# Rotary embedding of a two-layer decoder trunk: the half-head exchange by SBUF transfers instead of a TensorE product

## The chip, the cores and the metric

One core of a Trainium2 chip runs the whole program in one launch. The metric is the device time of one execution in microseconds (us), here the median of several executions. Engines are called as the profile calls them: PE (TensorE matmul) and PEld (its weight loads), DVE (VectorE), ACT (ScalarE), POOL (GpSimd), SP (SyncE); SPq and ACTq are the DMA issues that SP and ACT make.

## What is computed

Two layers of a hybrid decoder on a sequence of 256 tokens, D_MODEL 1024, all in float32. Each layer projects x by one matrix `w_in`, feeds three token mixers (a short convolution, attention with rotary positions, an RWKV-7 delta rule), gates and sums them, projects by `w_out`, normalises, and adds a feed-forward part (dense in layer 0, eight experts with the top two per token in layer 1). What matters here is the rotary step on the queries and the keys, eight heads of 64 channels each:

```python
def rope(x, pos):                       # x: (B, T, heads, 64)
    half = HEAD_DIM // 2                # 32
    inv = ROPE_THETA ** (-jnp.arange(half) / half)
    ang = pos[:, None] * inv[None, :]
    cos, sin = jnp.cos(ang), jnp.sin(ang)
    x1, x2 = x[..., :half], x[..., half:]
    return concatenate([x1 * cos - x2 * sin, x2 * cos + x1 * sin], -1)
```

Every channel needs its partner 32 channels away in the same head, times a sine, with a minus sign in the first half of the head.

## The kernel before, in words

**Layout.** Activations of the mixers lie with channels on the partitions and tokens along the free dimension, so a tile of 128 partitions holds two heads, and the two halves of a head are two neighbouring quarters of 32 partitions. Queries and keys are the tiles 0 to 7 of `share` ([128, 12, 256]); a step of the rotary embedding treats two tiles, `share[:, 2s:2s+2, :]` (128x512), and there are four steps, s = 0 to 3, in each of the two layers.

**Projections.** A float32 product is made of three products of fp32r parts: `mm3` (L503 to L505) multiplies high by low, low by high and high by high. The weights of each unit (128x2048) come by two SP loads into one of three `raw` buffers; ACT copies them to `w_hi` (`split_hi`, L1292), DVE subtracts to get `w_lo` (`split_lo`, L1801), and PE may then use them. SP loads the next unit into a `raw` buffer when its `w_lo` is made.

**The order of the work.** It is written out by hand in `TIMELINE` (L138 to L178), a list of steps such as ("front", "qkv", 2). Each engine walks the same list and runs its own handler for a step, if it has one; PE, DVE and ACT each work strictly in that order and meet by semaphores. "front" and "back" are the two halves of one projection unit on PE; on ACT "front" is `split_hi` of the unit two further on and, for gate-like units, the copy of the first bank; "back" copies the result out of PSUM. On DVE "front" is `split_lo` of the unit two further on (for ("qkv", 3) it is in "back", `LATE_LOW`, L181). Between these halves lie the small steps of the mixers. Those near the change:
- `decayed(1)` (ACT L1419, two copies into `ar`), at the end of the line of qkv unit 1.
- `mean(0)` and `var(0)` of the RWKV group norm: PE L895; DVE L1990 centres (`centred`), after that line's `split_lo`; ACT L1440 squares (`ysq_ready`); PE L730 sums the squares in `var`; ACT L1445 takes the root, DVE L1996 the reciprocal; `scaled(0)` is PE L739 (spreads it over channels) and DVE L2003, L2006, L2010.
- `bonus(1)`: DVE L1934, then ACT L1453.
- `scores(1, c)`: PE L783, whose second half, c = 1, waits for the first DVE masks (L1946) of c = 0; four L1946 on DVE for each c. `compact(1)`: ACT L1465, two copies, after the eighth mask.
- `att_scores(0)`: PE L933 and L935, which wait for `rope_ready` of the fourth rotary step; DVE L2025 follows.

**The rotary step.** PE (L913 to L921): one product of `rot` (a 128x128 matrix of 0, 1 and -1 in the constants) with the 128x512 of `share`, in float32, into the PSUM bank `E`. It waits for the rotary step before (bank `E` and its reader), the first for `tok_ready`. DVE (L2012 to L2019): `t4` = `E` times sine (L2017), `share` = `share` times cosine (L2018), sum (L2019), which counts `rope_ready`. ACT has no part in it. The buffers `t1`, `t2`, `t4` (128x512 each: `t_a`, `t_r`, `t_g` in the profile) are those of the RWKV rates and decays; `t4` is last read in `prep(1)` on DVE, `t1` and `t2` in `decayed(1)` on ACT.

**Waits on ACT.** Each `wait_ge` stands on its own before the instruction; a `dma_start` on ACT is issued from the same instruction stream as ACT's activations.

## Time and profile before

| what | value |
|---|---|
| median of 3 runs | 1683.87 us (1683.61 to 1684.73) |
| profiled execution: span, first to last instruction | 1682.6 us |
| its own time | not listed apart from the span |
| PE busy | 1656.3 us, 98% of the span, 10650 matmuls |
| PEld / DVE / ACT / POOL busy | 83% / 76% / 60% / 0% |
| mean granted TensorE clock | 0.993 of 2.4 GHz |
| DMA queue of SP / ACT | 400.97 MB / 8.82 MB |

How to read it: PE is busy nearly throughout, so time is gained where PE does less or waits less, and lost where something makes PE wait. Busy shares of the other engines are averages over stages with different limits and say little about one place; for that the chain of waits and the order of time around the place are read. The rotary steps lie at 180 to 206 us (layer 0) and 713 to 739 us (layer 1).

### The profile page before, as it was taken

The page shows a single profiled execution, that of the slowest core. Times are in us where ns is not written, and L with a number is a line of the kernel's source. Part 1 is how long each engine was busy: PE and PEld are TensorE (multiplying, and loading weights), DVE is VectorE, ACT ScalarE, POOL GpSimd, SP SyncE. Part 2 cuts the span into 40 slices and gives each one's busy share as a digit, 9 for nine tenths or more (in the row PEclk, how much of TensorE's full clock was granted, in tenths as well). Part 3 has the DMA queues.
Part 4 walks back from the last instruction along what each step waited for, and adds up shares of the span by engine and source line. Part 5 has one row for each costly group of instructions (what it writes and reads, how often), then busy time and mean ns, then how long its engine had stood idle before and what let it go on. Part 6 is the DMA issues. An engine that isn't in the chain of part 4 may idle for free.

```text
span 1682.6 us, 27509 instructions
## 1 busy us (share of the span) xinstructions
PE 1656.3 (98%) x10650; PEld 1402.5 (83%) x10650; DVE 1273.1 (76%) x1226; ACT 1001.9 (60%) x968; POOL 2.9 (0%) x12
## 2 busy tenths in 40 slices
PE   9999999999999999999999999999999999999997
PEld 8988788778887998978888888888888888888885
DVE  5766775664446668496478899898988889898987
ACT  6554463454444645444446777777776777777775
POOL 0000000000000000000000000000000000000000
PEclk9999999999999999999998999999999999999999
DMA  9433333556564543334376999999999999998993
GB/s 295 137 116 126 125 126 101 204 166 199 175 199 150 188 144 109 113 125 127 101 255 236 364 353 384 325 373 330 393 336 373 364 335 394 328 367 322 392 374 143
DMA packets 216185, 411.04 MB, mean 244 GB/s; under 512 B 9376, under 2 KB 83488, under 8 KB 215584
## 3 DMA queue, kind: packets, MB, share of 16 engines
q1 hardware_dynamic: 213840, 400.97, 67.5%
q10 hardware_dynamic: 2256, 8.82, 1.4%
q8 instruction: 63, 1.03, 0.3%
q14 instruction: 26, 0.21, 0.0%
HBM read 407.66 MB, written 2.10 MB: 244 GB/s over the span
## 4 chain that ended last, share of the span: by engine, by line
PE 93%; DVE 4%; issue 1%; ACT 1%; DMA 0%; SPq 0%; DVEq 0%; ACTq 0%
PE W L503 20%; PE W L505 19%; PE W L504 19%; PE Y L503 7%; PE Y L504 7%; PE Y L505 7%; PE Y L796 4%; PE W L701 1%; DVE w_lo L1801 1%; PE Y L701 1%; PE Y L783 1%; PE E L708 0%; DMA raw<-w_in 0%; PE Y L1072 0%; PE Y L1073 0%
## 5 line engine op out<-in xcount | busy, mean ns | idle before, releaser
L503 PE MATMUL W<-w_lo,x_hi 128*128 128x512 f32 (+1 forms) x1168 | 452.8, 388 | 1.5 <-DVE x_lo L2115 0.9
L505 PE MATMUL W<-w_hi,x_hi 128*128 128x512 f32 (+1 forms) x1168 | 442.2, 379 | 0.0
L504 PE MATMUL W<-w_hi,x_lo 128*128 128x512 f32 (+1 forms) x1168 | 441.5, 378 | 0.0
L1801 DVE TENSOR_TENSOR w_lo<-raw,w_hi 128x2048 fp32r<-128x2048 f32 x112 | 256.5, 2291 | 174.0 <-ACT w_hi L1292 172.7
L1808 DVE TENSOR_TENSOR w_lo<-raw,w_hi 128x2048 fp32r<-128x2048 f32 x144 | 329.6, 2289 | 45.6 <-ACT w_hi L1298 45.6
L1298 ACT ACTIVATE w_hi<-raw 128x2048 fp32r<-128x2048 f32 x144 | 276.1, 1917 | 72.6 <-PE Y L505 40.0
L1808 DVE TENSOR_TENSOR w_lo<-raw_more,w_hi 128x2048 fp32r<-128x2048 f32 x120 | 275.0, 2291 | 28.3 <-ACT w_hi L1298 27.6
L1298 ACT ACTIVATE w_hi<-raw_more 128x2048 fp32r<-128x2048 f32 x120 | 230.5, 1921 | 64.8 <-PE W L505 42.0
L1292 ACT ACTIVATE w_hi<-raw 128x2048 fp32r<-128x2048 f32 x112 | 214.2, 1913 | 81.6 <-PE W L505 47.8
L503 PEld LDWEIGHTS W<-w_lo,x_hi 128*128 128x128 f32 x1168 | 219.9, 188 | 45.0 <-issue 4.5
L505 PEld LDWEIGHTS W<-w_hi,x_hi 128*128 128x128 f32 x1168 | 219.7, 188 | 42.0
L504 PEld LDWEIGHTS W<-w_hi,x_lo 128*128 128x128 f32 x1168 | 220.1, 188 | 39.4 <-issue 1.0
L503 PE MATMUL Y<-w_lo,o_hi 128*128 128x512 f32 x440 | 172.2, 391 | 0.7 <-DVE o_lo L2128 0.7
L504 PE MATMUL Y<-w_hi,o_lo 128*128 128x512 f32 x440 | 171.3, 389 | 0.0
L505 PE MATMUL Y<-w_hi,o_hi 128*128 128x512 f32 x440 | 171.3, 389 | 0.0
L503 PE MATMUL W<-x_lo,w_hi 128*128 128x256 f32 x536 | 157.4, 294 | 3.0 <-DVE w_lo L1791 2.5
L504 PE MATMUL W<-x_hi,w_lo 128*128 128x256 f32 x536 | 152.0, 284 | 0.0
L505 PE MATMUL W<-x_hi,w_hi 128*128 128x256 f32 x536 | 151.9, 283 | 0.0
L503 PEld LDWEIGHTS W<-x_lo,w_hi 128*128 128x128 f32 x536 | 103.0, 192 | 7.1 <-issue 3.6
L504 PEld LDWEIGHTS W<-x_hi,w_lo 128*128 128x128 f32 x536 | 103.1, 192 | 0.3
L505 PEld LDWEIGHTS W<-x_hi,w_hi 128*128 128x128 f32 x536 | 103.1, 192 | 0.0
L503 PEld LDWEIGHTS Y<-w_lo,o_hi 128*128 128x128 f32 x440 | 82.6, 188 | 17.6 <-DVE w_lo L1801 1.2
(332 smaller groups left out, 1853.3 us busy)
## 6 DMA issues: line engine op xcount, KB each, us to landing
raw<-w_in SPq DMA_DIRECT2D x123, 512.0 KB, 4.6
raw<-moe_gate SPq DMA_DIRECT2D x48, 1024.0 KB, 6.4
raw<-moe_up SPq DMA_DIRECT2D x48, 1024.0 KB, 7.0
raw<-moe_down SPq DMA_DIRECT2D x48, 1024.0 KB, 5.7
raw_more<-moe_gate SPq DMA_DIRECT2D x40, 1024.0 KB, 7.5
raw_more<-moe_up SPq DMA_DIRECT2D x40, 1024.0 KB, 7.1
raw_more<-moe_down SPq DMA_DIRECT2D x40, 1024.0 KB, 6.3
raw<-w_branch SPq DMA_DIRECT2D x24, 512.0 KB, 4.5
```

The costliest lines, as they stand in the source:

```text
L503: nc.tensor.matmul(out_ap, lhs[0], rhs[1], start=start, stop=False)
L504: nc.tensor.matmul(out_ap, lhs[1], rhs[0], start=False, stop=False)
L505: return nc.tensor.matmul(out_ap, lhs[0], rhs[0], start=False, stop=stop)
L701: return nc.tensor.transpose(out_ap, in_ap, ident)
L783: last = nc.tensor.matmul(Y[(1 + u + h) % 4][:, part], keys[rows, m, tc], ar[rows, m, c].rearrange("p s t -> p (s t)"), start=True, stop=True)
L796: last = nc.tensor.matmul(tiles(bank, 4)[half, u, :], left[half, 4 * c + u, :], right[half, 4 * c + u, :], start=True, stop=True)
L1292: A(w_hi[u % 3][:], raw[u % 3][:], ACT.Copy).then_inc(hi_done, 1)
L1298: A(w_hi[(u + x) % 3][:], landing(place_of(x))[:], ACT.Copy).then_inc(hi_done, 1)
L1801: V.tensor_tensor(w_lo[u % 3][:], raw[u % 3][:], w_hi[u % 3][:].bitcast(F32), ALU.subtract)\
L1808: V.tensor_tensor(w_lo[r][:], landing(place_of(x))[:], w_hi[r][:].bitcast(F32), ALU.subtract).then_inc(lo_done, 1)
```

## The change

PE's `rope` goes. ACT gets a step `swap(s)`, four per layer, each with four SBUF to SBUF transfers of 32 partitions by 512 float32 (64 KB each): quarter i of the buffer `SWAPPED[s]` gets quarter i^1 of `share[:, 2s:2s+2, :]`. DVE's `rope` multiplies that buffer by the sine in place (no PSUM bank any more), and the minus sign is put once, in layer 0, step 0, into the sine table: two instructions on 32 partitions by 256. `swap(0)`, `swap(1)`, `swap(2)` and `swap(3)` stand in the list after `decayed(1)`, before `var(0)`, before ACT's `split_hi` of ("front", "qkv", 4), and before that of ("front", "qkv", 5).

```diff
@@ TIMELINE
-    ("front", "qkv", 1), ("cu", 0, 1), ("back", "qkv", 1), ("cy", 0, 1), ("yrow", 0), ("decayed", 1),
-    ("front", "qkv", 2), ("mean", 0), ("back", "qkv", 2), ("var", 0), ("tok", 1),
-    ("front", "qkv", 3), ("scaled", 0), ("bonus", 1), ("back", "qkv", 3), ("rope", 0), ("scores", 1, 0),
-    ("front", "qkv", 4), ("scores", 1, 1), ("compact", 1), ("back", "qkv", 4), ("rope", 1),
+    ("front", "qkv", 1), ("cu", 0, 1), ("back", "qkv", 1), ("cy", 0, 1), ("yrow", 0), ("decayed", 1), ("swap", 0),
+    ("front", "qkv", 2), ("mean", 0), ("back", "qkv", 2), ("swap", 1), ("var", 0), ("tok", 1),
+    ("front", "qkv", 3), ("scaled", 0), ("bonus", 1), ("back", "qkv", 3), ("swap", 2), ("rope", 0), ("scores", 1, 0),
+    ("front", "qkv", 4), ("scores", 1, 1), ("compact", 1), ("back", "qkv", 4), ("rope", 1), ("swap", 3),
@@ shared by the engines
+        SWAPPED = (t4, t1, t2, t4)
+        QUARTERS = [slice(a, a + HD // 2) for a in range(0, P, HD // 2)]
@@ tensor engine
-            def rope(l, s):
-                wait_jobs(pe, l * MIX_JOBS + JOB0["qkv"] + s + 1)
-                if s:
-                    pe.wait_ge(sem("rope_ready"), 4 * l + s)
-                else:
-                    pe.wait_ge(sem("tok_ready"), 2 * l + 2)
-                nc.tensor.matmul(E[:], rot, share[:, 2 * s:2 * s + 2, :].rearrange("p m t -> p (m t)"),
-                                 start=True, stop=True).then_inc(sem("rot_done"), 1)
@@ scalar engine
+            def swap(l, s):
+                wait_jobs(act, l * MIX_JOBS + JOB0["qkv"] + s + 1)
+                if s < 3:
+                    act.wait_ge(sem("decayed_ready"), 2 * l + 2)
+                    act.wait_ge(sem("prep_ready"), 2 * l + 2)
+                else:
+                    act.wait_ge(sem("rope_ready"), 4 * l + 1)
+                for i, to in enumerate(QUARTERS):
+                    act.dma_start(SWAPPED[s][to], share[QUARTERS[i ^ 1], 2 * s:2 * s + 2, :]).then_inc(sem(f"swapped{s % 3}"), 16)
@@ vector engine, rope(l, s)
-                dve.wait_ge(sem("rot_done"), 4 * l + s + 1)
-                V.tensor_tensor(t4[:], tiles(E[:]), sin, ALU.mult)
+                other = SWAPPED[s]
+                if l == 0 and s == 0:
+                    dve.wait_ge(sem("cst_full"), 96)
+                    for quarter in QUARTERS[0::2]:
+                        last = V.tensor_scalar(cst[quarter, C_SIN:C_END], cst[quarter, C_SIN:C_END], -1.0, None, ALU.mult)
+                    link(last)
+                dve.wait_ge(sem(f"swapped{s % 3}"), 64 * (l + 1) if s in (1, 2) else 64 * (2 * l + 1 + s // 3))
+                V.tensor_tensor(other[:], other[:], sin, ALU.mult)
                 link(V.tensor_tensor(src, src, cos, ALU.mult))
-                mark(V.tensor_tensor(src, t4[:], src, ALU.add), "rope_ready", 4 * l + s + 1)
+                mark(V.tensor_tensor(src, other[:], src, ALU.add), "rope_ready", 4 * l + s + 1)
```

## Rows read from the trace of the kernel before

**Rows 1.** The page, part 4: the chain that ended last, shares by engine.
```profile
PE 93%; DVE 4%; issue 1%; ACT 1%; DMA 0%; SPq 0%; DVEq 0%; ACTq 0%
```

**Rows 2.** PE in order of time, second rotation: start us, us, engine, line, operation.
```profile
190.97 0.39 PE L505 MATMUL W<-w_hi,x_hi 128*128 128x512 f32 x1
191.20 1.02 PE L920 MATMUL E<-share,cst 128*128 128x512 f32 x2
...
192.29 0.40 PE L504 MATMUL W<-w_hi,x_lo 128*128 128x512 f32 x1
```

**Rows 3.** Chain of waits, 177 to 188 us: start us, us, what.
```profile
177.00 0.70 DVE mc L2003
...
180.08 2.29 DVE w_lo L1801
...
184.33 0.70 DVE sc L1946
...
187.26 1.13 PE Y L783 x8
```

**Rows 4.** DVE in order of time, 195 to 202 us; brackets: idle before, releaser.
```profile
195.66 2.29 DVE L1801 TENSOR_TENSOR w_lo<-raw,w_hi 128x2048 fp32r<-128x2048 f32 x1 [1.30 <-ACT w_hi L1292]
...
201.15 2.29 DVE L1801 TENSOR_TENSOR w_lo<-raw,w_hi 128x2048 fp32r<-128x2048 f32 x1 [1.28 <-ACT w_hi L1292]
```

**Rows 5.** PE in order of time, the first attention scores.
```profile
206.02 0.49 PE L933 MATMUL Y<-share 64*128 64x128 f32 x4 [1.07 <-DVE share L2019]
```

**Rows 6.** ACT and its DMA issues (ACTq) in order of time, 861 to 863 us.
```profile
861.81 0.59 ACT L1529 ACTIVATE x_hi<-W 128x512 fp32r<-128x512 f32 x1
861.84 0.38 ACTq L1535 DMA_DIRECT2D xtok<-x_spill  x1
862.26 0.49 ACTq L1537 DMA_DIRECT2D cmo<-const_moe  x1
862.28 1.92 ACT L1292 ACTIVATE w_hi<-raw 128x2048 fp32r<-128x2048 f32 x1
862.78 0.45 ACTq L1538 DMA_DIRECT2D rt_s<-router  x1
```

**Rows 7.** SP's issues in order of time: a run of small loads.
```profile
15.34 0.62 SPq L382 DMA_DIRECT2D cm<-const  x1
```

**Rows 8.** ACT in order of time, 163 to 170 us.
```profile
163.83 0.62 ACT L1419 ACTIVATE ar<-t_r 128x512 f32<-128x512 f32 x1
164.35 1.90 ACT L1292 ACTIVATE w_hi<-raw 128x2048 fp32r<-128x2048 f32 x1
169.33 0.63 ACT L1440 ACTIVATE xn<-mc 128x512 f32<-128x512 f32 x1 [3.08 <-DVE mc L1990]
```

**Rows 9.** DVE in order of time: the same split in layer 0 and in layer 1.
```profile
166.28 2.29 DVE L1801 TENSOR_TENSOR w_lo<-raw,w_hi 128x2048 fp32r<-128x2048 f32 x1 [7.73 <-ACT w_hi L1292]
...
699.56 2.29 DVE L1801 TENSOR_TENSOR w_lo<-raw,w_hi 128x2048 fp32r<-128x2048 f32 x1 [7.73 <-ACT w_hi L1292]
```

**Rows 10.** PE's weight loads in order of time: the sums of squares in `var(0)`.
```profile
170.15 0.98 PEld L730 LDWEIGHTS Y<-cst,xn 128*128 128x128 f32 x8
```

**Rows 11.** ACT in order of time, 170 to 176 us: the root of `var(0)`.
```profile
172.38 0.27 ACT L1445 ACTIVATE inv<-Y,small 128x8 f32<-128x8 f32 x1
```

**Rows 12.** ACT in order of time, 181 to 194 us.
```profile
181.37 1.90 ACT L1292 ACTIVATE w_hi<-raw 128x2048 fp32r<-128x2048 f32 x1
192.34 1.27 ACT L1465 ACTIVATE ac<-sc 64x512 f32<-64x512 f32 x2 [9.07 <-DVE sc L1946]
193.64 1.92 ACT L1292 ACTIVATE w_hi<-raw 128x2048 fp32r<-128x2048 f32 x1
```

**Rows 13.** DVE in order of time: a pair of scalar products over 256 columns.
```profile
141.06 0.62 DVE L1921 TENSOR_SCALAR t_g<-t_g,prm 128x256 f32<-128x256 f32 x2
```

**Rows 14.** DMA issues by line: KB each, median us from issue to landing.
```profile
prm<-par SPq DMA_DIRECT2D x1, 86.0 KB, 8.4
```

**Rows 15.** Busy us by stretch: PE, PEld, DVE, ACT, POOL; granted clock, DMA share, GB/s.
```profile
880.00:890.00 10.00, 10.00 (x49) 8.99 (x49) 7.13 (x18) 8.43 (x10) 0.00 (x0) 0.63 0.00 0
```

More of the change, by code:

```diff
@@ L1229, in _ @@
                         "spread": spread, "tok": tok, "scores": scores, "invert": invert, "mx": mx, "dx": dx, "cg": cg, "cu": cu,
-                        "cy": cy, "mean": mean, "var": var, "scaled": scaled, "rope": rope,
+                        "cy": cy, "mean": mean, "var": var, "scaled": scaled,
                         "att_scores": att_scores, "probs_t": probs_t, "att_out": att_out}
@@ L1706, in _ @@
                         "exps": exps, "ksq": ksq, "knorm": knorm, "decayed": decayed, "tok": tok, "bonus": bonus, "invert": invert,
-                        "mx": mx, "compact": compact, "cg": cg, "cu": cu, "yrow": yrow, "mean": mean, "var": var,
+                        "swap": swap, "mx": mx, "compact": compact, "cg": cg, "cu": cu, "yrow": yrow, "mean": mean, "var": var,
                         "softmax": softmax, "probs_t": probs_t, "att_out": att_out, "osplit": osplit, "msplit": msplit,
```

## The prediction, made before the changed kernel was run

> **What bounds the kernel now.** I read the shares of the chain that ended last first: PE carries 93% of it, DVE 4% [rows 1]. So a change counts where it shortens PE's work on that chain, or where it makes PE wait. The shares cannot say which of the two holds at the rotary steps; that takes the order of time around them. In layer 0 there are two stretches. From 177 to 187 us the chain runs over DVE: `scaled(0)`, the bonus, a weight split, rotary step 0, four masks, and only then PE's second half of `scores(1, 1)` [rows 3]. From there it is PE's own work, with rotations 1 and 2 in it, until the first attention scores, before which PE sat idle for 1.07 us for the fourth rotary sum [rows 5]. Layer 1 repeats this 533.3 us later [rows 9].
>
> **What goes: eight products on PE.** Around rotation 1 the last product before it starts at 190.97 and the second after it at 192.29 [rows 2], 1.32 us apart. Starts of undisturbed products of 512 columns lie 0.23 us apart (190.97 to 191.20 [rows 2]), so two steps would be 0.46, and a rotation costs PE 0.86 us. Eight make 6.9 us, 0.4% of the run. Of these I count:
> - Rotation 0 (both layers): nothing. It stands ahead of `scores(1, 0)`, but PE's next point on the chain, at 187.26, waits for DVE's masks, and those come one after the other on DVE from 177.00 on, with no PE in between [rows 3]. PE only waits longer.
> - Rotations 1 and 2: 2 x 0.86 = 1.72 us earlier on PE, rotation 3 another 0.86; but the next meeting point is the fourth rotary sum on DVE [rows 5]. It hangs on two weight splits with a rotary step between them: 195.66 and 201.15, before which DVE was idle for 1.30 and 1.28 us, waiting for ACT's high part [rows 4]. The first high part (ACT 193.64) comes right after the masks and `compact(1)` [rows 12], so PE's gain does not move it. The second waits for PE's last qkv product, which does come 1.72 us earlier. So the second split can start 1.28 us earlier at most, then DVE is the bound. That is the whole gain on offer: at most 1.28 us a layer, and rotation 3 is worth nothing.
>
> **What comes: sixteen transfers a layer on ACT's stream.** ACT's issues are taken from [rows 6]: 861.84, 862.26, 862.78, and the third ends at 863.23, so 1.39 us for three, 0.46 each; four take 1.84 us. ACT's own next work waits behind them. The same rows say when they start: 861.84 is 0.03 us after the ACTIVATE of 861.81 began, while the next ACTIVATE, earlier in the program than the issues, ran only at 862.28. So issues pass behind work already handed to the engine, and hide under it. Bounds for one issue: 0.38, the first of the run [rows 6], and 0.62, SP in a run of small loads [rows 7]; four, with 0.04 between, make 1.6 to 2.6 us. I take 1.84, ACT's own.
> - **swap(0)** waits for `decayed_ready`, the end of the copy before it, 163.83 + 0.62 = 164.45 [rows 8]. So nothing hides it. The issues run from 164.47 to 166.31, and `split_hi` starts then and not at 164.35: 1.96 us late. Behind it, in order: the split on DVE (it had been idle 7.73 us for this high part [rows 9]), `centred` behind that split, and ACT's square (idle 3.08 us for `centred` [rows 8]), which ended at 169.96. PE began to load these squares as weights at 170.15 [rows 10]. With 0.05 us for the signal the slack is 0.14 us. So PE now stands for 1.96 - 0.14 = 1.82 us in `var(0)`. Nothing takes it back: the chain from there to 177.00 is PE's, then DVE's. Two layers: **+3.64 us**. By the bounds of an issue the stall is 1.6 to 2.6 us.
> - **swap(1)** (1.84 us) stands ahead of the root. The root ran at 172.38 [rows 11]; its reciprocal is first needed by PE's spread about 1.05 us before 177.00 [rows 3], near 175.9. Since PE itself is 1.8 us late, slack is about 2.9 us after 0.5 us for root and reciprocal are in. Hidden; uncovered only if an issue took over 0.7 us.
> - **swap(2)** delays a `split_hi` of 181.37 [rows 12] by 1.84. DVE takes that unit after the four masks, at 187.2 [rows 3]; 1.90 us of work from 183.2 ends at 185.1. Hidden by 2.1 us.
> - **swap(3)** can be issued once the second of the two copies of `compact(1)` is handed over, just after 192.34 [rows 12]: from 192.36 to 194.20. `split_hi` starts 0.56 us later than 193.64. The first split and rotary step 2 go with it, so the gain at the second split is 1.28 - 0.56 = 0.72 us. If the issues start only when the second copy runs, 0.64 later, 0.1 us is left; with issues of 0.62 us, none. Two layers: **-1.44 us**, bounds -1.9 (issues of 1.6 us in all) and +0.2.
> - **Landing.** swap(0) to swap(2) are issued at least 10 us before DVE reads them; swap(3) by 194.20, read at about 203.3. The longest landing of a small transfer, 86 KB, took 8.4 us from issue, in the crowded start [rows 14]; even that fits. No trace row has SBUF as the source. Taken as nothing.
> - SP's queue is not passed by anything; its loads that wait for the late splits move 0.6 to 2 us and have over 10 us to their use. Of the other queues POOL's is untouched.
>
> **The sign.** In layer 0, step 0, DVE does two products on 256 columns and waits for their end, on the chain of [rows 3]. A pair of that kind took 0.62 us [rows 13] on 128 partitions; on 32 I know no row, so 0.4 (if fewer partitions help) to 0.7. Taken 0.65 with the wait: **+0.65 us**, once. The first rotary product now reads SBUF and not PSUM; like its neighbours it is 128x512 and counted as equal.
>
> **Sum.** 3.64 + 0.65 - 1.44 = +2.85 us. The profiled execution has a span of 1682.6; no other time is listed for it, and the median of the runs is 1.27 us above it. What lies around the span does not change, so the sum is added to the median: 1683.87 + 2.85 = **1686.7 us**, +0.17%. A measurement of this kernel tells 0.2% (3.4 us) from no change. The bounds by terms: low 1.6 x 2 + 0.4 - 1.9 = +1.7 (1685.6), high 2.6 x 2 + 0.7 + 0.2 = +6.1 (1690.0).
>
> **A rule that speaks against the stall.** The Trainium skill, "DMA: Bandwidth & Descriptors", section "Issuing engines are not separate DMA queues", says that the time a sequencer takes to start a DMA is usually small beside the DMA itself. Read as a reason to count the issues as nothing, it would take out both the stall and the 0.56 us; [rows 6] and the 0.14 us of slack speak against it here.
>
> **Rivals.**
> - **A: the issues cost ACT nothing.** Then no stall, and the full 1.28 us a layer: 0.65 - 2.56 = -1.9, 1682.0 us. For it: issues do pass behind running work [rows 6]. Against: swap(0)'s own wait leaves ACT empty. Chance 5%.
> - **B: PE gets its 0.86 us back for every rotation,** because DVE's chain is not as tight as it looks: -6.9 + 0.65 = -6.2, 1677.6 us, faster. Against: the two meeting points of [rows 3, 5]. Chance 3%.
> - **C: long issues, slower.** Place: swap(0) in both layers. Small transfers of 32 rows go at 0.62 us an issue as in [rows 7]: four with gaps 2.6 us, stall 2.6, gain of swap(3) gone: +6.0, 1689.9 us. It crosses the 0.2% when an issue takes over 0.49 us (each 0.01 more costs 0.16 over both layers, stall and swap(3) together). For it: so close to 0.46. Chance of being past that point 31%.
> - **D: the clock.** PE's waits grow: 1.8 us in `var(0)`, then products of 2 columns, and before the attention scores from 1.07 [rows 5] to 1.07 + 3 x 0.86 - 0.72 = 2.9 us. In the router stage, where PE ran mostly products of 8 columns, the granted clock averaged 0.63 over 10 us [rows 15], so part of it at the 1.2 GHz level. If one such drop of about 7 us came in each layer, half of it is lost: +7 on top, 1693.7 us. Against: full-width products on either side of both waits. Chance 8%. The Trainium skill, "TensorE: Matmul & The Clock Gate", section "HAM oscillation — how this bites in real kernels", makes idle gaps the cause of such drops; no row here shows a gap alone doing it.
> - **E: the transfers land late or are not used:** a wait on `swapped` before step 3. It decides only if landing takes over 9 us from issue; +0.5 to 2. Chance 3%.
>
> **How the numbers follow.** My forecast, a net of +1.7 to +3.4, has 50%. With most of A and a third of E inside the 0.2% band (1680.5 to 1687.2), no change comes to 0.55; slower (C, D, the rest of E) to 0.41; faster (B and the rest of A) to 0.04. The predicted time is that of the likeliest case, 1686.7. The range for 8 in 10: 1684.0, which leaves A and B out, to 1690.3, which holds C and leaves D out.
>
> **What the profile after would show.** L920 gone, 16 matmul records fewer, 32 new ACTq rows of about 0.4 us. After `decayed(1)` four issues, then `split_hi` near 166.3 and PE's L730 with an idle of about 1.8 us, released by ACT L1440, in both layers. DVE's first mask at 184.33 + 1.8 + 0.65 in layer 0 and without the 0.65 in layer 1. Before L933 PE idle for about 2.9 us, released by DVE's sum, and the distance from the eighth mask to L933 0.7 us shorter. `swapped` never the last releaser. I am wrong if L730 does not wait (A), if the distance from masks to scores shrinks by over 1.28 us (B), if issues last 0.6 us (C), or if the granted clock falls in 170 to 210 us (D).

## The result and the profile after

| | before | after |
|---|---|---|
| median | 1683.74 us (4 runs, 1682.77 to 1684.73) | 1698.53 us (4 runs, 1698.16 to 1698.97) |
| ratio | | 1.0086, 95% interval 1.0073 to 1.0098 |
| span of the profiled execution | 1682.6 us | 1696.8 us |
| mean granted TensorE clock | 0.993 | 0.988 |
| PE busy, matmuls | 1656.3 us, 10650 | 1657.3 us, 10634 |

The change costs 14.8 us, 0.9%. It was forecast at 1686.7 with a range up to 1690.3, so even the range is missed. PE has 16 records fewer and is busy 1 us longer: its work went down and each piece of it took longer somewhere. The page's chain says where else to look: PE fell from 93% to 90%, "issue" rose from 1% to 2%, and ACT's queue from nothing to 1%.

```profile
PE 90%; DVE 5%; issue 2%; ACT 2%; ACTq 1%; DMA 0%; SPq 0%; DVEq 0%
```

The order of time on ACT and its queue, layer 0, answers to [rows 8] and [rows 11]:

```profile
164.40 0.62 ACT L1412 ACTIVATE ar<-t_r 128x512 f32<-128x512 f32 x1
165.21 3.06 ACTq L1501 DMA_DIRECT2D t_g<-share  x4
168.37 1.92 ACT L1285 ACTIVATE w_hi<-raw 128x2048 fp32r<-128x2048 f32 x1 [3.35 <-issue]
...
174.07 1.90 ACTq L1501 DMA_DIRECT2D t_a<-share  x3
176.00 1.28 ACT L1438 ACT_TABLE_LOAD   x1 [1.52 <-issue]
```

The same place in layer 1:

```profile
705.57 0.62 ACT L1412 ACTIVATE ar<-t_r 128x512 f32<-128x512 f32 x1
706.37 2.47 ACTq L1501 DMA_DIRECT2D t_g<-share  x4
708.95 1.92 ACT L1285 ACTIVATE w_hi<-raw 128x2048 fp32r<-128x2048 f32 x1 [2.76 <-issue]
```

Before, `split_hi` started 0.52 us after the start of the second copy [rows 8]. Now it starts 3.97 us after it (164.40 to 168.37): 3.45 us late in layer 0, and by the same reckoning 2.86 in layer 1 (705.57 to 708.95, less 0.52). The four issues are 3.06 and 2.47 us of that. The rest is 0.3 us before the first and 0.1 behind the last.

PE's two longest waits, as the groups of waits have them (engine, result and line <- who was waited for: us in total, times, longest). The one in `var(0)` is new, the one before the attention scores grew from 1.07 us [rows 5]. Below them PE's rows at the wait of `var(0)` in either layer (L733; [rows 10]) and at the attention scores in layer 0 (L926):

```profile
PE Y L926 <- DVE share L2029: 7.9, 2, 4.0
PE Y L733 <- ACT xn L1433: 5.5, 2, 3.1
```

```profile
174.05 1.86 PE L733 MATMUL Y<-cst,xn 128*128 128x2 f32 x8 [3.05 <-ACT xn L1433]
...
179.55 0.41 PE L507 MATMUL W<-x_hi,w_lo 128*128 128x256 f32 x1
179.76 0.41 PE L508 MATMUL W<-x_hi,w_hi 128*128 128x256 f32 x1
...
180.51 0.28 PE L507 MATMUL W<-x_hi,w_lo 128*128 128x256 f32 x1
180.63 0.28 PE L508 MATMUL W<-x_hi,w_hi 128*128 128x256 f32 x1
...
213.56 0.49 PE L926 MATMUL Y<-share 64*128 64x128 f32 x4 [3.96 <-DVE share L2029]
...
714.63 1.05 PE L733 MATMUL Y<-cst,xn 128*128 128x2 f32 x8 [2.46 <-ACT xn L1433]
```

Look at the durations. The eight products at 174.05 take 1.86 us, and those at 714.63 take 1.05. After the first, products of 256 columns start 0.21 us apart until about 180, then 0.12. That is the clock, as the windows of this trace say (the last but two column is the granted clock, in parts of 2.4 GHz; 0.50 is the 1.2 GHz level):

```profile
174.00:180.00 6.00, 5.95 (x22) 4.81 (x23) 0.20 (x1) 2.46 (x4) 0.00 (x0) 0.50 0.70 216
180.00:186.00 6.00, 6.00 (x57) 5.70 (x57) 2.16 (x4) 2.46 (x3) 0.00 (x0) 0.99 0.00 0
214.00:217.00 3.00, 3.00 (x17) 2.06 (x14) 2.44 (x8) 0.00 (x0) 0.00 (x0) 0.54 0.47 180
716.00:719.00 3.00, 3.00 (x12) 2.28 (x11) 0.20 (x1) 1.65 (x3) 0.00 (x0) 0.50 1.00 355
754.00:757.00 3.00, 3.00 (x9) 2.42 (x8) 2.93 (x9) 0.00 (x0) 0.00 (x0) 0.51 0.08 29
```

Four stretches at 1.2 GHz that the trace of before does not have (there the windows 160 to 180, 200 to 220, 700 to 720 and 740 to 760 us all stand at 1.00). Each starts within 1.5 us of the end of one of PE's four waits, the first already in the last 0.7 us of its wait. The first lasts about 7 us, the other three about 3.5. PE is called busy all through them, which is why its busy share hides the loss.

A third wait of PE grew as well, for the masks before the second half of `scores(1, 1)` (L786 here): from 0.2 to 1.25 us in layer 0, which is the "PE only waits longer" of the prediction. No low stretch follows it.

**Where the 14.2 us of span are.** DVE does the same work in both traces, so the distance of a row from its twin before is the delay at that point. Four of DVE's rows, layer 0:

```profile
183.77 0.69 DVE L2007 TENSOR_TENSOR mc<-mc,Y 128x512 f32<-128x512 f32 x1 [5.91 <-PE Y L742]
189.07 0.57 DVE L2024 TENSOR_SCALAR cst<-cst 32x256 f32<-32x256 f32 x2
204.43 2.29 DVE L1805 TENSOR_TENSOR w_lo<-raw,w_hi 128x2048 fp32r<-128x2048 f32 x1 [2.68 <-ACT w_hi L1285]
208.69 2.29 DVE L1805 TENSOR_TENSOR w_lo<-raw,w_hi 128x2048 fp32r<-128x2048 f32 x1
```

- 177.00 [rows 3] is now 183.77, 6.77 late. Of this 0.6 came from the start of the run (it differs by up to 4 us between traces, see below), 3.3 is the stall (3.45 less the slack of 0.14), and the remaining 2.9 is the clock.
- The sign takes 0.6 (189.07 to 189.68): 7.4.
- The second weight split, 201.15 [rows 4], is at 208.69: 7.54. The rotations' removal was to bring it 0.72 forward. It gave nothing, as the split before it now waits 2.68 us, not 1.30, for the high part that stands behind swap(3).
- A split at 232.16 before comes at 240.36: 8.2, and 8.4 further on. So the clock behind the attention scores took about 0.9.
- Layer 1 in the same way: 2.9 for the stall by the split at 710.90 (699.56 before, [rows 9]), so 11.3; 1.5 to 1.7 for the clock by 723.11 (710.28 before), so 12.8; 0.1 by the second split; 1.2 for the clock behind the scores, so 14.2.

Together: stalls 6.0 us, clock 6.7, sign 0.6, the second splits +0.3, start of the run 0.6. The clock's share is a difference between delays, not a row of its own, and the experiments test it. One more place must be kept in mind for them: the router stage (before: about 882 to 897 us) has a low stretch of 14 us in both traces, and the delay is the same ahead of it and behind it, 14.1 and 14.2 us.

### The profile page after: what moved, and what is told of

Read it like the earlier page. It is cut to its first block, busy times and chain, and to the rows that moved or that the text cites. A ratio compares the mean times of both kernels' runs of the same rounds, so it can differ in the third digit from the quotient of the medians.

```text
span 1696.8 us, 27512 instructions
## 1 busy us (share of the span) xinstructions
PE 1657.3 (98%) x10634; PEld 1406.0 (83%) x10634; DVE 1273.9 (75%) x1228; ACT 1002.6 (59%) x968; POOL 2.9 (0%) x12
## 4 chain that ended last, share of the span: by engine, by line
PE 90%; DVE 5%; issue 2%; ACT 2%; ACTq 1%; DMA 0%; SPq 0%; DVEq 0%
PE W L506 19%; PE W L508 18%; PE W L507 18%; PE Y L506 7%; PE Y L508 7%; PE Y L507 7%; PE Y L799 4%; PE W L704 1%; DVE w_lo L1805 1%; DVE sc L1950 1%; ACT w_hi L1285 1%; PE Y L704 1%; ACTq L1501 1%; PE Y L786 0%; PE E L711 0%
```

## The experiments

Each was timed against the kernel before on the same chip; "delay" is again the distance of a DVE row from its twin in the trace of before. Before stood at 1684.08 beside experiments 1, 2, 3 and 8, at 1683.87 beside 5, 6, 7 and 9, and at 1684.21 beside 4, 10 and 11.

**1. No transfers.** DVE multiplies whatever the buffers hold: the exchange of quarters is left out, the three DVE instructions and the sign stay.

```diff
 def swap(l, s):                      # scalar engine
 ...
-                for i, to in enumerate(QUARTERS):
-                    act.dma_start(SWAPPED[s][to], share[QUARTERS[i ^ 1], 2 * s:2 * s + 2, :]).then_inc(sem(f"swapped{s % 3}"), 16)
 def rope(l, s):                      # vector engine
 ...
-                dve.wait_ge(sem(f"swapped{s % 3}"), 64 * (l + 1) if s in (1, 2) else 64 * (2 * l + 1 + s // 3))
+                dve.wait_ge(sem("decayed_ready"), 2 * l + 2)
```

> Leaves the exchange out: no SBUF transfers, the sine multiplies what lies in the buffers; PE's rotations stay gone, the sign stays. My theory after the result: the loss comes from ACT's issues (0.61 us each, not 0.46), which hold PE in var(0) by 3.3 and 2.7 us, and from four stretches at the 1.2 GHz level that follow PE's waits (2.9, 0.9, 1.65 and 1.25 us by the shifts between the two traces). Without transfers no wait in var(0), so 1683.7 + 0.6 (sign) - 2 x 1.28 = 1681.8 us if the clock holds before the attention scores, about 1684 if it falls there. The rival, that the products on PE kept it busy and their removal alone brings the clock down, says: the clock falls in 206 to 220 us here too, and the time is 1684 or more.

Measured: 1684.10 us (10 runs, 1681.99 to 1685.35), ratio 0.9998 (0.9988 to 1.0007). So the sixteen transfers a layer, with all that follows from them, are the whole 14 us (whether it is their issue or their traffic is settled by experiment 8). But the other half is as telling: without transfers the kernel should have been faster by the two times 1.28 us of [rows 4], less the sign. It isn't. The order of time on PE and DVE before the attention scores, layer 0:

```profile
201.52 2.29 DVE L1803 TENSOR_TENSOR w_lo<-raw,w_hi 128x2048 fp32r<-128x2048 f32 x1
...
206.40 0.49 PE L926 MATMUL Y<-share 64*128 64x128 f32 x4 [2.58 <-DVE share L2027]
...
208.86 0.63 PE L507 MATMUL W<-w_hi,o_lo 128*128 128x512 f32 x1
209.28 0.63 PE L508 MATMUL W<-w_hi,o_hi 128*128 128x512 f32 x1
```

The split no longer waits: the delay was 1.60 us on the way there (1.0 of it from the start of the run, 0.6 the sign) and is 0.37 at 201.52, so the gain of 1.23 is there. PE, with 2.6 us less to do, then waits 2.58 us instead of 1.07, and its next products start 0.43 us apart and not 0.23. After that the delay is 1.60 again. Layer 1 does the same: 1.68 ahead of the two splits, 0.43 at the second, 1.73 behind the scores, with a low stretch from 740 to 743.5 us. What DVE gained, the clock took. This is the outcome that the expectation gave to its rival for that place: the removal of the products is enough to bring the clock down there, by way of the longer wait and without any transfer.

**2. The sign in the constants.** Two edits: the two `tensor_scalar` of the vector engine go, and the host lays the table out with its signs.

```diff
-                if l == 0 and s == 0:
-                    dve.wait_ge(sem("cst_full"), 96)
-                    for quarter in QUARTERS[0::2]:
-                        last = V.tensor_scalar(cst[quarter, C_SIN:C_END], cst[quarter, C_SIN:C_END], -1.0, None, ALU.mult)
-                    link(last)
...
-    general = np.concatenate([general, np.tile(np.cos(ang), (4, 1)), np.tile(np.sin(ang), (4, 1))], 1)
+    general = np.concatenate([general, np.tile(np.cos(ang), (4, 1)), np.concatenate([-np.sin(ang), np.sin(ang)] * 2)], 1)
```

> The changed kernel with the minus sign in the constant table and not made by DVE. My theory: exactly the two products (0.57 us and a signal) leave the chain: 1698.5 - 0.6 = 1697.9 us. The rival: at that point PE waits anyway through another path, and nothing changes: 1698.5.

Measured: 1698.68 us (4 runs), ratio 1.0083 (1.0066 to 1.0100), the same as the changed kernel. The 0.6 us are gone from DVE's order, but behind the attention scores of layer 0 the low stretch was twice as long as in the changed kernel:

```profile
211.00:218.00 7.00, 5.00 (x21) 3.79 (x22) 5.73 (x14) 1.32 (x2) 0.00 (x0) 0.54 0.47 150
```

The four issues of layer 0's first group took 2.53 us here and not 3.06, so this trace lacks a second half microsecond, and still ends later. So what was saved on the path was lost again to the clock in this trace. With one trace it can't be said whether that is the rule.

**3. PE kept running in both waits.** Idle products (128x256, into a bank that nobody reads) before either wait, nothing else. They can't take the stall away.

```diff
 def var(l, p):
+                if p == 0:
+                    keep_running(6)
                 pe.wait_ge(sem("ysq_ready"), 2 * l + p + 1)
 def att_scores(l, part):
                 if part == 0:
+                    keep_running(8)
                     pe.wait_ge(sem("rope_ready"), 4 * l + 4)
```

> The changed kernel, with idle products on PE into the free bank E: six ahead of the wait in var(0), eight ahead of the wait for the attention scores (some 0.45 us each, so 2.7 and 3.6 us, inside the waits of 2.5 to 3.1 and 4.0 us). My theory: the waits stay, the clock stays at 2.4 GHz in all four places, and 6.7 us come back: 1691.8 us. The rival, that the slow stretches cost nothing because DVE and ACT are the bound there, says 1698.5 us with the clock high.

Measured: 1690.06 us (7 runs, 1689.33 to 1691.14), ratio 1.0033 (1.0021 to 1.0044): 8.5 us less than the changed kernel, by doing more work on the busiest engine. The windows at the four places, in the same columns as above:

```profile
174.00:180.00 6.00, 5.42 (x39) 4.47 (x38) 0.84 (x2) 3.80 (x7) 0.00 (x0) 1.00 0.77 219
206.00:212.00 6.00, 5.49 (x27) 4.37 (x26) 5.86 (x8) 3.19 (x2) 0.00 (x0) 1.00 0.77 230
707.00:713.00 6.00, 6.00 (x41) 5.46 (x40) 2.98 (x2) 2.18 (x3) 0.00 (x0) 1.00 0.18 40
739.00:745.00 6.00, 6.00 (x28) 5.03 (x27) 5.93 (x5) 3.40 (x4) 0.00 (x0) 1.00 0.46 145
```

This shows the clock's share at the four places: none of the low stretches is left, and ahead of the router stage the delay is 8.5 us, 1.8 of it from the start of the run, against 14.1 with 0.6. That is 6.8 us less, where the sum above has 6.7. The rest of the gain in this trace is not at the four places: in the router stage, whose low stretch was 14 us in before and after and 7 us here, the delay falls from 8.5 to 6.5. So the 6 us by which this kernel is still slower than before are the stalls, the sign and the second splits (6.9 together), less what the router stage gave, with the scatter of the start.

**4. PE kept running at the first place only**, `keep_running(6)` in `var` alone.

> The changed kernel with six idle products on PE ahead of its wait in the first variance product alone. Against the changed kernel (1698.5): if the clock falls only for the wait in front of it, the low stretches at 174 to 181 and 716 to 720 us go (2.9 + 1.65 = 4.5 us), those before the attention scores stay, the stall itself (3.3 + 2.7) stays: median 1693 to 1695. If the two places are coupled, the second goes too and it comes near the 1690.1 with both filled.

Measured: 1695.32 us (4 runs, 1694.95 to 1695.80), ratio 1.0067 (1.0052 to 1.0083), 3.2 us less than the changed kernel and just outside the expected 1693 to 1695. The low stretches behind `var(0)` are gone, and the row of 183.77 stands at 181.00. But in layer 1 PE's wait before the scores grew to 4.74 us and the low stretch behind it from 3.5 to 7 us:

```profile
747.00:753.00 6.00, 4.26 (x19) 3.20 (x20) 4.75 (x11) 0.31 (x1) 0.00 (x0) 0.50 0.52 175
```

It cost 1.9 us of delay there and not 1.2. The two shares don't simply add: filling both is worth 8.5, and the first alone 3.2.

**5. PE's eight products kept**, as products of constants of the same size; the changed kernel else.

```diff
@@ tensor engine; its entry in the list of handlers comes back too
+            def rope(l, s):
+                wait_jobs(pe, l * MIX_JOBS + JOB0["qkv"] + s + 1)
+                if s:
+                    pe.wait_ge(sem("rope_ready"), 4 * l + s)
+                else:
+                    pe.wait_ge(sem("tok_ready"), 2 * l + 2)
+                nc.tensor.matmul(E[:], rot, cst[:, 0:512], start=True, stop=True)
```

> The changed kernel with a product of the same size in the place of each rotation (constants as data, into the idle bank, nobody reads it): transfers, sign and ACT's stream as in the changed kernel, PE's work as before. If PE's freed time is what makes it stand long enough before the attention scores for the clock to fall: the wait there is 1.5 to 2.5 us and not 4.0, no stretch at 1.2 GHz at 214 to 218 and 754 to 757 us; against the changed kernel 0.9 + 1.25 less, and up to 1.3 a layer more for the rotations' own time at the second split: median 1696.5 to 1699. The stall in the first variance product and the clock behind it (3.3 + 2.9 and 2.7 + 1.65 us) stay. If the rotations' removal does not bear on the clock: 1699 or more with the low stretches still there.

Measured: 1693.72 us (4 runs, 1692.71 to 1696.44), ratio 1.0060 (1.0045 to 1.0076), 4.8 us less than the changed kernel and below the expected 1696.5 to 1699. PE's waits and the two places before the attention scores:

```profile
PE Y L733 <- ACT xn L1442: 5.9, 2, 3.4
...
PE Y L935 <- DVE share L2038: 1.8, 2, 0.9
```

```profile
209.00:215.00 6.00, 5.00 (x27) 3.48 (x28) 5.60 (x7) 1.78 (x1) 0.00 (x0) 1.00 0.83 277
743.00:749.00 6.00, 5.91 (x24) 4.05 (x22) 5.93 (x8) 1.95 (x2) 0.00 (x0) 1.00 0.59 185
```

The waits before the scores are 0.9 us and not 4.0, and the clock holds; that is the 2.1 us (0.9 and 1.2) which the low stretches behind them had cost. The second split comes where it came in the changed kernel (209.16 against 208.69, with the delay in front of it 0.5 greater), so eight products more on PE cost nothing there. **At this place the work that was saved on PE was worth less than nothing**: it turned into a wait, and the wait into a lower clock. The rest, and the reason why it came out better than expected, is not due to the eight products as far as is shown. In layer 1 the clock did not fall behind a wait of 2.46 us in `var(0)`, and in the changed kernel it did, behind 2.46 too (some 1.6 us). And in the router stage the delay falls from 10.8 to 8.6 us, with a low stretch of 7 us and not 14.

**6. swap(0) alone moved** on ACT's stream, to where nobody waits closely.

```diff
-    ("front", "qkv", 1), ("cu", 0, 1), ("back", "qkv", 1), ("cy", 0, 1), ("yrow", 0), ("decayed", 1), ("swap", 0),
-    ("front", "qkv", 2), ("mean", 0), ("back", "qkv", 2), ("swap", 1), ("var", 0), ("tok", 1),
+    ("front", "qkv", 1), ("cu", 0, 1), ("back", "qkv", 1), ("cy", 0, 1), ("yrow", 0), ("decayed", 1),
+    ("front", "qkv", 2), ("mean", 0), ("back", "qkv", 2), ("swap", 1), ("var", 0), ("tok", 1), ("swap", 0),
```

> The changed kernel with swap(0) alone moved on ACT's stream, from behind decayed(1) to behind tok(1). If the loss sits in swap(0)'s place: PE's wait in the first variance product is gone (it had 3.05 and 2.46 us), and so is the low clock at 174 to 181 and 716 to 720 us: 6.2 us less in layer 0, 4.3 in layer 1, median near 1688. If every place of four issues costs ACT's readers the same: the stall shows up elsewhere (the root, scaled or the first bonus) and the median stays above 1694.

Measured: 1688.28 us (10 runs, 1686.21 to 1691.52), ratio 1.0026 (1.0017 to 1.0035), as expected to 0.3 us. PE does not wait in `var(0)`, and the clock stands at 1.00 there in both layers. So ten of the 14.8 us went with the place of one group of four issues. That the forecast was so close is partly luck: the low stretch before the scores of layer 1 was 7 us here and not 3.5, and in the router stage the delay fell by 2.5 us (5.7 to 3.2), which no one had counted. What is left is the sign and the attention waits, still 3.95 and 3.94 us (2.58 without transfers, experiment 1), as swap(3) keeps DVE late, with the clock behind them.

**7. Other shapes of transfer**, to find why an issue takes 0.61 us and not 0.46.

```diff
 for i, to in enumerate(QUARTERS):    # step 3 is as it was
+                    c = slice(64 * i, 64 * i + 64)
+                    if s == 0:
+                        a, b = SWAPPED[s][:, :, c], share[:, 2 * s:2 * s + 2, c]
+                    elif s == 1:
+                        a, b = SWAPPED[s][to], w_branch[l, 0:32, 0:512].rearrange("p (m t) -> p m t", m=2)
+                    elif s == 2:
+                        a, b = SWAPPED[s][to, 0, :], share[QUARTERS[i ^ 1], 2 * s, :]
 ...
+                    act.dma_start(a, b).then_inc(sem(f"swapped{s % 3}"), 16)
```

The exchange is left out in steps 0 and 1 and for half of step 2, so this kernel is for the durations of the issues alone.

> The changed kernel with other shapes of its transfers, four a step still: step 0 moves 128 rows by 64 columns of each token half, rows kept (same bytes, four times the rows, a quarter of the run length); step 1 reads 32 rows of the branch weights in HBM and not SBUF; step 2 moves 32 rows but one token half, half the bytes; step 3 is as it was. The exchange is left out in steps 0 and 1 and half of step 2. If an issue's time goes with the number of runs or rows: step 0 over 0.61 us, step 2 under. If it goes with SBUF as source: step 1 under 0.5 and the others 0.6. If it is a constant of ACT's queue in a group of four: all 0.5 to 0.6, and the first 0.46 came from groups of three with work beside them.

Measured: 1698.43 us (one run). The DMA issues of one line, by tile (ns min, median, max), first of the changed kernel, then of this one, with the group of step 0 in layer 1 below:

```profile
L1501 ACTq DMA_DIRECT2D t_g<-share x16: 514/612/1147, 165.2 to 740.4; - x16
L1501 ACTq DMA_DIRECT2D t_a<-share x8: 515/612/614, 173.5 to 715.9; - x8
```

```profile
L1510 ACTq DMA_DIRECT2D t_g<-share x16: 515/626/1337, 165.2 to 741.0; - x16
L1510 ACTq DMA_DIRECT2D t_a<-w_branch x8: 349/441/444, 173.9 to 716.0; - x8
L1510 ACTq DMA_DIRECT2D t_r<-share x8: 595/612/618, 187.3 to 728.8; - x8
...
706.67 2.72 ACTq L1510 DMA_DIRECT2D t_g<-share  x4
```

`t_r`, half the bytes: 0.61 as before. `t_g` mixes step 0, with four times the rows, and step 3, as it was; the group of step 0 in layer 1 took 2.72 us and not 2.47, so the rows added 0.06 us an issue. `t_a`, same destination, same bytes, source in HBM and not SBUF: 0.44, and 0.35 for the first. **With the destination in SBUF the source made the difference.** The rows on which the forecast of 0.46 rested all had HBM as the source.

SBUF as the source is not dear by itself, though. The trace of before has four issues that store from SBUF to HBM, one on ACT and three on SP, at 0.33 to 0.39 us. The one on ACT:

```profile
L1362 ACTq DMA_DIRECT2D x_spill<-xtok x1: 391/391/391, 581.7 to 581.7; - x1
```

The 0.6 us belong, as far as these runs go, to transfers with SBUF at both ends. They are not the only dear ones: SP's small loads of [rows 7], from HBM into 64 partitions, took 0.62 each. What an issue spends the time on is open. What made the fourth issue of layer 0's first group take 1.15 us (1.34 here) is open; SP issued nothing in that time.

**8. SP issues the transfers**, the sign in the table. Swaps 0 to 2 stand behind the load of the second unit of branch 0, swap 3 behind the first of gate 1.

```diff
@@ sync engine; swap itself moves here from the scalar engine, with sp in the place of act
                         for q in range(n):
                             load_rows(u + q, 0, w_branch[l, :, q * 512:(q + 1) * 512], where * BR, BT)
+                            if where == 0 and q == 1:
+                                for s in range(3):
+                                    swap(l, s)
 ...
                             load_rows(u + q, 0, w_in[l][:, c:c + 512], 512 * (q % 2), 4)
+                            if kind == "gate1" and q == 0:
+                                swap(l, 3)
```

> The same sixteen transfers a layer, but issued by SP where it waits anyway (steps 0 to 2 after the load of the second unit of branch0, step 3 after the first of gate1), sign in the table. My theory: ACT's stream is free, no wait in var(0), the transfers land long before DVE reads them: 1683.7 - 2 x 1.28 = 1681.2 us if the clock holds before the attention scores, about 1683.3 if it falls. The rival, that it is the transfers' traffic and landing and not the issuing engine, says it stays near 1698.

Measured: 1683.31 us (10 runs, 1681.58 to 1685.92), ratio 0.9992 (0.9982 to 1.0002). The 14.8 us are gone, and nothing is gained. The same sixteen transfers a layer still run, so their traffic and their landing were not the cost; what cost was that ACT issued them, ahead of work that PE waits for. (0.6 of the 14.8 us is the sign, now in the table.) SP's queue in the order of time:

```profile
171.52 2.49 SPq L407 DMA_DIRECT2D t_g<-share  x4
...
176.77 2.41 SPq L407 DMA_DIRECT2D t_r<-share  x4
184.26 0.38 SPq L352 DMA_DIRECT2D raw<-w_in  x1
```

Four issues take SP 2.4 us too; it has them to spare, since its next load comes 5 us after the last of them. PE waits 2.58 us before the attention scores in both layers. Behind it the clock fell in layer 0 and not in layer 1:

```profile
207.00:210.00 3.00, 3.00 (x18) 2.09 (x17) 1.92 (x6) 0.33 (x1) 0.00 (x0) 0.50 0.48 186
738.00:744.00 6.00, 3.89 (x26) 3.10 (x27) 5.45 (x13) 2.83 (x2) 0.00 (x0) 1.00 0.56 180
```

The delay says what that is worth. In layer 0 it is 1.81 us ahead of the splits, 0.58 at the second, 1.81 again behind the scores: gained and lost. In layer 1, with the same edit and the same wait, it is 2.04, then 0.78, and stays there.

**9 and 10. The same with PE kept running before the attention scores**, `keep_running(8)` and then `keep_running(5)` as in experiment 3.

> The run sp_sign with eight products of 256 columns on PE (0.22 us each, 1.8 us in all) ahead of its wait for the fourth rotary sum, where PE stood for 2.6 us. If the clock gives back the gain of the removed rotations: no stretch at the 1.2 GHz level at 207 to 211 us, the 1.2 us a layer at the second weight split (201.15) are kept through the attention scores, and the median is 1681 to 1682.5, that is 1.5 to 2.5 below sp_sign and the kernel before. If the gain is lost for another reason (DVE's own order, weight loads): no change against sp_sign, 1683 to 1684.

Measured: 1683.45 us (11 runs, 1682.57 to 1685.49), ratio 0.9998 (0.9989 to 1.0007). No low stretch at either place, yet no gain that can be told from none: the size of the filler was wrong in the expectation. Eight products took 3.62 us, 0.45 each, and DVE waited 1.20 us for the first scores where before it was 0.38 (L2025 there), so 0.8 of the 1.24 us was given back.

> sp_sign_fill with five products ahead of the fourth rotary sum and not eight. Eight took 3.62 us (736 to 739.5 us), 0.45 us each and not the 0.22 expected there, and DVE then waited 1.20 us for the first scores in layer 0 where it had waited 0.38 before: they overshot by 0.8 us a layer. Five are 2.26 us, which ends ahead of the sum. If the clock is all that gives the gain back: no low stretch around 207 and 740 us, the first attention scores 1.2 us a layer earlier than in the kernel before, median 1681.0 to 1682.3. If a remaining wait of 0.5 us is enough for the clock to fall, or the gain is lost further on: 1683 to 1684.5, no change.

Measured: 1682.46 us (11 runs, 1680.68 to 1684.58), ratio 0.9986 (0.9977 to 0.9995). The only version whose interval lies below 1, and just above the expected range. PE at the place, and the windows of both layers:

```profile
205.94 2.32 PE L529 MATMUL E<-s_s 128*128 128x256 f32 x10
208.67 0.49 PE L943 MATMUL Y<-share 64*128 64x128 f32 x4 [0.40 <-DVE share L2030]
```

```profile
205.00:211.00 6.00, 5.60 (x35) 4.29 (x34) 5.52 (x10) 3.20 (x2) 0.00 (x0) 1.00 0.74 263
738.00:744.00 6.00, 5.59 (x35) 4.29 (x34) 5.48 (x12) 3.19 (x2) 0.00 (x0) 1.00 0.63 211
```

The delay falls by 1.24 us at the second split in layer 0 and by 1.26 in layer 1 (201.15 and 734.46 before), and stays down both times. That is the 1.28 us a layer of the prediction, reached with the issues and the clock out of the way, and it is read from rows. Neither the span nor the median shows it by itself. This trace, of the slowest of the eleven runs, was 3.9 us late by 67 us, and its router stage gave back 1.9. The median is 1.75 us below that of before, which could hold the gain of the router stage as well as that of the splits. And an interval that ends at 0.9995, one of eleven, is weak evidence that the kernel is faster at all.

**11. The transfers still on ACT**, with the repairs of 2, 3 (second place) and 6 together.

> The changed kernel with its transfers still on ACT's queue: swap(0) behind tok(1), sign in the table, eight idle products ahead of the attention scores. If the shares add up: 1688.3 less 0.6 for the sign less what the low clock at 209 to 212 and 741 to 748 us took, 2 to 4: median 1684 to 1686, so no or a small loss against before. If the clock finds another place (longer low stretch elsewhere, as with the sign alone): 1687 or more.

Measured: 1685.78 us (10 runs, 1684.57 to 1687.33), ratio 1.0010 (1.0000 to 1.0019). Within the expected range: the shares add up here, and what remains of the loss is at the edge of what can be told from none. Before the attention scores the clock stood at 1.00. From 166 us to the router stage the delay grows by only 0.5 us (2.0 to 2.5), and there it falls to 0.3.

## Why the prediction was wrong, point by point

- **What bounds the kernel: right.** The two meeting points held. PE waited in `var(0)` and before the attention scores, for the releasers that were named. PE's own 0.86 us per rotation was worth nothing (experiment 5), and the 1.28 us a layer that were on offer exist (experiments 8 and 10).
- **The term "four take 1.84 us": mis-sized.** Four issues took 2.47 us on ACT (3.06 once) and cost 0.4 more around them. The stall was 3.3 and 2.7 us, not 1.82 each: +6.0 in place of +3.64. The prediction had both prices in front of it, 0.46 and 0.62, and took ACT's own because the engine matched. What mattered was what lies at the two ends (experiment 7), which it touched only for the landing, with "No trace row has SBUF as the source". That is not so: four issues of the trace before read SBUF, at 0.33 to 0.39 us. What no row has is SBUF at both ends. A kind of transfer that no row has makes every price of an issue a bound, not only the one that comes to mind.
- **The gain of 1.44 us: gone, as its own bound said.** "With issues of 0.62 us, none" is what came: the second splits are 0.1 to 0.15 us later per layer.
- **The sign: right**, 0.6 against 0.65.
- **swap(1) and swap(2) hidden, landing nothing: right.** swap(1) holds ACT's load of a function table (ACT_TABLE_LOAD) 1.52 us and does not come up among PE's waits. Landing took 1.9 to 5.1 us from issue. The issuing page of the Trainium skill ("DMA: Bandwidth & Descriptors", section "Issuing engines are not separate DMA queues") calls the issue time usually small beside the DMA; here 0.61 us stands against a landing of 2.1 at the median. It is the smaller of the two, which is of no help: the cost lay in what stood behind the issues on ACT.
- **Rival C had the mechanism and 31%, and 1689.9.** By it alone the kernel would have come to +6.6 or so (stalls 6.0, sign 0.6), near its upper bound of 1690. Experiment 3, with the clock held at the four places, measured 1690.06; some 2 us of the router stage are in that, so the agreement is closer than the reasoning deserves.
- **Rival D is the step that failed.** It was priced as an alternative, at 8%, with "full-width products on either side of both waits" against it. The products are there, and they did not hold the clock. It fell behind both waits, in both layers, and took some 6.7 us in the trace; experiment 3, which held it, won 8.5 us in the medians (6.8 at the four places by its trace). It was also not independent: once the stall is longer, and PE has less work before the scores, both waits grow (to 3.05, 2.46, 3.96 and 3.96 us). D belonged on top of C, and even on top of the forecast itself: that had a wait of 2.9 us before the scores, and in experiment 1 a wait of 2.58 brought the clock down in both layers. With C and D together the prediction's own figures give 1689.9 + 7 = 1697, against 1698.5 measured, a sum made with the result in hand. The rule that was cited beside it (the Trainium skill, "TensorE: Matmul & The Clock Gate", section "HAM oscillation — how this bites in real kernels"), that idle gaps of PE bring such drops, is borne out by experiments 3 and 4, where the filled gaps have no drop behind them. And "no row here shows a gap alone doing it" overlooked the start of the trace before, where a wait of 2.54 us has a low stretch with it, from 12.2 to 15.7 us (PE in order of time, and the window):

```profile
12.54 0.58 PE L503 MATMUL W<-x_lo,w_hi 128*128 128x256 f32 x1 [2.54 <-DVE w_lo L1791]
...
12.00:16.00 4.00, 3.46 (x17) 3.47 (x18) 3.44 (x4) 2.80 (x3) 0.00 (x0) 0.57 1.10 345
```

## What to carry to other kernels

On a kernel whose tensor engine is 98% busy, work that is removed from it turns into a wait unless what it waits for moves too; where such a wait reached some 2.5 us here, or 1.4 us with very small products behind it, the clock could fall, and it took back as much as was saved (experiment 1) or more. So price a new wait of the tensor engine twice, once for its length and once for the half speed behind it, and try a few idle products in front of it: here they were worth 7 to 8.5 us. They must end before what PE waits for arrives: eight of them overshot by 0.8 us, five did not (experiments 9 and 10).
Before putting DMA issues on a compute engine's stream, look for what stands behind them; four cost 2.5 us there and nothing on a queue that was idle. Take their price from a row with the same kind of memory at both ends.

## What the runs showed of the hardware

- **Issue time depends on what lies at the two ends.** ACT: 0.61 us from SBUF to SBUF, 0.44 from HBM to SBUF (first of a group 0.52 and 0.35), at the same destination and size; 0.39 from SBUF to HBM. SP: 0.59 from SBUF to SBUF, 0.37 and 0.47 for its weight loads from HBM, 0.33 to 0.37 for its stores to HBM, but 0.62 for small loads from HBM to 64 partitions. Half the bytes changed nothing, four times the rows with a quarter of the run added 0.06.
- **The clock in a dense kernel.** Waits of PE amid full-width products, and what the granted clock did behind them: 0.40 us (experiment 10), 0.9 (5), 1.07 (before) and 1.25 (the masks, after) no fall; 2.46 a fall (after and 2, layer 1) or none (5, layer 1); 2.52 a fall (2, layer 0); 2.58 a fall in both layers of experiment 1 but only in layer 0 of 8; 2.7, 3.05, 3.4 and each from 3.9 up (after, 2, 4, 5, 6, 7) a fall. Each fall was to the 1.2 GHz level, for about 3.5 or 7 us. So between 2.46 and 2.58 us the same wait went both ways, and what decides is open. The wait alone does not decide: far from the edit, at 42 us in layer 0, waits of 1.38 us (experiment 3) and 1.73 (10) had a fall behind them, where eight products of 2 columns follow; in the trace of before PE does not wait there, and the clock holds.

```profile
41.76 1.18 PE L733 MATMUL E<-cst,t_d 128*128 128x2 f32 x8 [1.38 <-ACT t_g L1383]
```

- **A low stretch can move.** Taking one away left or lengthened another (experiment 4; in 2, which takes none away, one was longer). The router stage's, 14 us long before and after, was about 7 us in experiments 3, 5, 6, 9, 10 and 11, and the delay fell there by 1.9 to 2.5 us in each. Whether that follows from these edits or changes from one execution to the next was not tried.
- **The granted clock differs between executions of one kernel, and the time with it.** Of the 21 executions of the kernel before that stood beside experiments 4, 10 and 11, six had a mean clock of 0.992 or 0.993 and took 1685.16 to 1686.26 us; the fifteen with 0.994 to 0.996 took 1682.86 to 1684.83.
- **The start of a run wanders.** Between 10 and 70 us the traces of kernels that are identical there differ by up to 4 us in delay, in experiment 10 with a low clock from 43 to 50 us. A span of one trace therefore settles nothing under 4 us; rows around the place and medians do.
